# Running sums of a state-space scan sent through DRAM to all partitions, with the masks added on GpSimd

## What is computed

```python
def segsum_exp(a):
    cs = jnp.cumsum(a, axis=-1)
    diff = cs[..., :, None] - cs[..., None, :]
    mask = jnp.tril(jnp.ones((t, t), dtype=bool))
    return jnp.exp(jnp.where(mask, diff, -jnp.inf))
...
    xg = xs * dt[..., None]
    a = dt * a_neg
    cb = jnp.einsum('bclgn,bcsgn->bcgls', cc, bc)
    m_mat = cb[:, :, :, None] * segsum_exp(a)
    y_diag = jnp.einsum('bcgels,bcsgep->bclgep', m_mat, xg)
...
    y_off = jnp.einsum('bclgn,bcgepn,bcgel->bclgep', cc, prev_states, jnp.exp(a_cs))
    y = y_diag + y_off + d_skip * xs
    y = rmsnorm(y * silu(z), groups of 512) ; out = concat(attn, y) @ w_out
```

## Time and profile before

| | |
|---|---|
| median of 3 runs | 860.03 us (859.88 to 860.25) |
| profiled execution | 860.37 us |
| its span, first to last instruction | 858.3 us |
| PE busy | 850.3 us, 99% |
| PE weight loads busy | 707.6 us, 82% |
| DVE busy | 620.0 us, 72% |
| ACT busy | 534.6 us, 62% |
| POOL busy | 185.6 us, 22% |

### The profile page before, as it was taken

How to read it: one execution, slowest core, us unless ns; L and a number is a source line. 1 busy time by engine, 2 the same in 40 slices (tenths; PEclk the granted TensorE clock), 3 DMA queues, 4 the chain that set the end, 5 groups by cost and what they waited for, 6 DMA issues and landing times.

```text
span 858.3 us, 13054 instructions
## 1 busy us (share of the span) xinstructions
PE 850.3 (99%) x4645; PEld 707.6 (82%) x4645; DVE 620.0 (72%) x1125; ACT 534.6 (62%) x1031; POOL 185.6 (22%) x176
## 2 busy tenths in 40 slices
PE   9999999999999999999999999999999999999996
PEld 7877888778887888888888888877888888888885
DVE  6867866678776797778887546576797678877544
ACT  7668466765887864655565434787874655665432
POOL 0212053110152430023222000152330022222001
PEclk9999999999999999999999999999999999999999
DMA  9813563445434336655555555444336555555631
GB/s 316 293 56 127 178 203 130 148 147 176 157 139 147 110 140 217 203 177 185 195 190 178 222 196 172 151 147 141 107 145 220 186 185 196 189 177 180 230 107 50
DMA packets 94948, 146.21 MB, mean 170 GB/s; under 512 B 6564, under 2 KB 55204, under 8 KB 94884
## 3 DMA queue, kind: packets, MB, share of 16 engines
q1 hardware_dynamic: 92852, 139.58, 48.6%
q0 software_dynamic: 1296, 4.72, 1.7%
q10 hardware_dynamic: 736, 1.07, 0.3%
HBM read 144.32 MB, written 1.05 MB: 169 GB/s over the span
## 4 chain that ended last, share of the span: by engine, by line
PE 99%; issue 0%; POOL 0%; DVE 0%; ACT 0%; POOLq 0%; DVEq 0%
PE bank L1335 57%; PE bank L1291 17%; PE bank L1294 9%; PE bank L1217 6%; PE bank L1492 2%; PE bank L1420 1%; PE bank L1396 1%; PE bank L1393 1%; PE bank L1423 1%; PE bank L1222 0%; PE bank L1238 0%; PE bank L1236 0%; PE bank L1233 0%; PE bank L1482 0%; PE bank L1499 0%; PE bank L1460 0%
## 5 line engine op out<-in xcount | busy, mean ns | idle before, releaser
L1126 DVE TENSOR_TENSOR lo<-raw,hi 128x1024 fp32r<-128x1024 f32 x242 | 299.8, 1262 | 102.1 <-ACT hi L1511 101.7
L1511 ACT ACTIVATE hi<-raw 128x1024 fp32r<-128x1024 f32 (+1 forms) x258 | 266.7, 1058 | 126.8 <-PE bank L1335 68.2
L1335 PE MATMUL bank<-hi,xT 128*128 128x512 f32 (+2 forms) x800 | 252.0, 386 | 0.0
L1335 PEld LDWEIGHTS bank<-hi,xT 128*128 128x128 f32 x800 | 147.2, 188 | 30.9 <-issue 4.3
L1291 PE MATMUL bank<-xT,hi 128*128 128x512 f32 x640 | 171.8, 394 | 0.0
L1335 PE MATMUL bank<-lo,xT 128*128 128x512 f32 (+2 forms) x400 | 151.0, 378 | 0.0
L1291 PEld LDWEIGHTS bank<-xT,hi 128*128 128x128 f32 x640 | 110.6, 188 | 16.3
L1335 PE MATMUL bank<-hi,hT 128*128 128x512 f32 x348 | 107.8, 389 | 0.0
L1294 PEld LDWEIGHTS bank<-xT,lo 128*128 128x128 f32 x640 | 95.6, 189 | 11.9
L1294 PE MATMUL bank<-xT,lo 128*128 128x256 f32 x640 | 99.1, 281 | 0.0
L1335 PEld LDWEIGHTS bank<-lo,xT 128*128 128x128 f32 x400 | 75.4, 189 | 12.1
(11 more groups left out here) (284 smaller groups left out, 1119.0 us busy)
## 6 DMA issues: line engine op xcount, KB each, us to landing
raw<-in_w_in SPq DMA_DIRECT2D x26, 1024.0 KB, 4.9
raw<-in_w_gate SPq DMA_DIRECT2D x44, 512.0 KB, 3.7
raw<-in_w_up SPq DMA_DIRECT2D x44, 512.0 KB, 4.7
raw<-in_w_down SPq DMA_DIRECT2D x22, 1024.0 KB, 4.8
raw<-in_w_out SPq DMA_DIRECT2D x20, 1024.0 KB, 5.0
raw<-in_w_in_b SPq DMA_DIRECT2D x10, 1024.0 KB, 5.0
raw<-in_w_in_a SPq DMA_DIRECT2D x7, 1024.0 KB, 7.8
raw<-in_w_in_a SPq DMA_DIRECT2D x8, 256.0 KB, 5.2
```

Source lines behind the costliest of these rows:

```text
L1126: return engine.tensor_tensor(lo[r][:, cols], raw[c.i % RAW][:, cols], hi[r][:, cols].bitcast(F32), ALU.subtract)
L1335: last = nc.tensor.matmul(bank[:, 0:wd], still[a], mv[r][:, off:off + wd], start=c.first and i == 0 and j == 0, stop=(c.last or c.closes a ...
L1511: nc.scalar.activation(hi[c.i % SPLIT][:, cols], raw[c.i % RAW][:, cols], ACT.Copy)\
```

## The change

The negative running sums are kept as 16 rows in f32 (`csum`, now [16, 2, 128]; `sums` loses the three bf16 parts and writes the rows with one DVE operation, and `soft3` writes dt * a once instead of three times with zeros beside it). SP writes them to DRAM (`rows_out`, behind the products of `x0 + 512`), and reads them back with eight DMAs per layer (`spread`), each of which puts four rows on all 128 partitions: 256 KB into one of now eight buffers MT0 to MT7. Six of them are issued ahead of the products of `z0`, two within the first chunk of `z0 + 512`. SP waits for the write, for the last transposes of the attention, and for the last convolution transposes ahead of the seventh.

A new step `cap` on POOL adds a mask (`later`, bf16: zero or 1e30) to each buffer, 128 x 512 at a time: groups (0,0) and (0,1) in the chunks of `z0`, groups (1,1) and (1,0) in the second place of `z0 + 512`, which in the list is behind the first `xback` and ahead of the second. `decay` is then only ACT's exponential, in place in MT, with scale -1 and `ncs` as the bias. The decay matmuls, their turns in the ring of banks, `picks` and its setup on DVE go away.

```diff
+    def rows_spread(groups):
+
+        for g, m in groups:
+            for i in range(2):
+                scan["spread", g, m, i] = sc.step("spread", q=i, mg=(m, g), layer=layer, att=a, before=scan.get(("conv", 2, 1)))
+
+    def caps(g, m):
+
+        for i in range(2):
+            scan["cap", g, m, i] = sc.step("cap", q=i, mg=(m, g), of=scan["spread", g, m, i], sums=scan["sums"])
+
     def decays(g, m):
         for i in range(2):
-            bk = sc.bank()
-            s = sc.step("decay", q=i, mg=(m, g), bank=bk, sums=scan["sums"])
-            bk.freed = (s, "scalar")
-            scan["decay", g, m, i] = s
+            scan["decay", g, m, i] = sc.step("decay", q=i, mg=(m, g), of=scan["cap", g, m, i])
...
     b = halves(sc, w_in, [(x0 + 512, 512)], do(conv_silu, 0), att(2) + do(conv, 1, 0), do(conv, 1, 1))
+    sc.step("rows_out", layer=layer, sums=scan["sums"])
     evac_x(b, 2)
     sc.goes_on(att(3))
     scan["gain"] = sc.gain(("ssm_norm", layer))
-    b = halves(sc, w_in, [(z0, 512)], do(conv_silu, 1), do(conv, 2, 0) + do(bback),
+    rows_spread(((0, 0), (0, 1), (1, 1)))
+    b = halves(sc, w_in, [(z0, 512)], do(conv_silu, 1), do(caps, 0, 0) + do(caps, 0, 1) + do(conv, 2, 0) + do(bback),
                do(back, 0) + do(conv, 2, 1))
     scan["z", 0] = evacs(sc, b, "ev_z", j=0, kind_of="h")
     sc.goes_on(do(conv_silu, 2))
-    b = halves(sc, w_in, [(z0 + 512, 512)], do(decays, 0, 0) + do(weigh, 0, 0),
-               do(decays, 0, 1) + do(weigh, 0, 1), do(scanned, 0, 0) + do(back, 1) + do(low_at_once))
+    b = halves(sc, w_in, [(z0 + 512, 512)], do(rows_spread, ((1, 0),)) + do(decays, 0, 0) + do(weigh, 0, 0),
+               do(caps, 1, 1) + do(caps, 1, 0) + do(decays, 0, 1) + do(weigh, 0, 1), do(scanned, 0, 0) + do(back, 1) + do(low_at_once))
     ev_z1 = evacs(sc, b, "ev_z", j=1, kind_of="h", what="copy")
     sc.goes_on(do(squared, 0, 0) + do(decays, 1, 1) + do(scanned, 0, 1))
...
-    csum = keep("csum", [P, M, P], BF16)
-    picks = keep("picks", [P, SH, P], BF16)
+    decays = keep("decays", [P, 2, 4, P])
+    decay_rows = nc.dram_tensor("decay_rows", (2, SH, M, P), F32, kind="Internal").ap()
...
+                if s.kind == "rows_out":
+                    ended(sp, s.sums, "vector")
+                    sp.dma_start(decay_rows[s.layer], Hb["csum"][:, :, :]).then_inc(rows_stored, 16)
+                if s.kind == "spread":
+
+                    n, (m, g) = s.i % 8, s.mg
+                    if n == 0:
+                        sp.wait_ge(rows_stored, 16 * (s.layer + 1))
+                        for x in s.att["flip"][-3:]:
+                            ended(sp, x, "tensor")
+                    if n == 6:
+                        ended(sp, s.before, "tensor")
+                    hh = 8 * g + 4 * s.q
+                    sp.dma_start(Hb[f"MT{n}"][:, :, :], decay_rows[s.layer, hh:hh + 4, m].partition_broadcast(P))\
+                      .then_inc(spread_in[n], 16)
...
-                    last = nc.tensor.matmul(bank[0:96, 64 + m * P:64 + (m + 1) * P],
-                                            Hb["da"][:, m, :, :].rearrange("p a s -> p (a s)"), upper,
+                    last = nc.tensor.matmul(bank[0:SH, 64 + m * P:64 + (m + 1) * P], Hb["da"][:, m, :], upper,
                                             start=True, stop=True)
...
-            elif s.kind == "decay":
-                m, g = s.mg
-                ended(pe, s.sums, "scalar")
-                bank = freed(pe, s.bank)
-                if s.i == 0:
-                    pe.wait_ge(picks_made, 1)
-                for i in range(4):
-                    hh = 8 * g + 4 * (s.q % 2) + i
-                    last = nc.tensor.matmul(bank[:, i * P:(i + 1) * P], picks[0:KSEL, hh, :], csum[0:KSEL, m, :],
-                                            start=True, stop=True)
-                last.then_inc(sem["decay", "tensor"], 1)
...
-                act.wait_ge(sem["decay", "tensor"], s.i + 1)
-                if s.i >= 4:
-                    act.wait_ge(sem["diag", "tensor"], s.i - 3)
+                ended(act, s.of, "gpsimd")
                 for i in range(4):
                     hh = 8 * g + 4 * (s.q % 2) + i
-                    last = nc.scalar.activation(Hb[f"MT{s.i % 4}"][:, i, :], psum[4 + s.bank.at][:, i * P:(i + 1) * P],
-                                                ACT.Exp, bias=Hb["ncs"][:, m, hh:hh + 1])
+                    mt = Hb[f"MT{s.i % 8}"][:, i, :]
+                    last = nc.scalar.activation(mt, mt, ACT.Exp, scale=-1.0, bias=Hb["ncs"][:, m, hh:hh + 1])
                 done(last, s)
...
+            if s.kind == "cap":
+
+                m, g = s.mg
+                pool.wait_ge(spread_in[s.i % 8], 16 * (s.of.layer + 1))
+                ended(pool, s.sums, "vector")
+                mt = Hb[f"MT{s.i % 8}"][:, :, :]
+                nc.gpsimd.tensor_tensor(mt, mt, spread(Hb["later"][:, :].unsqueeze(1), [P, 4, P]), ALU.add)\
+                  .then_inc(sem["cap", "gpsimd"], 1)
...
-                copy, left = nc.vector.tensor_copy, bank[:, 64:64 + M * P].rearrange("p (m l) -> p m l", l=P)
-                chained(copy(csum[0:96, :, :], left[0:96]))
-                chained(tt(left[0:96], left[0:96], csum[0:96, :, :], ALU.subtract))
-                copy(csum[32:64, :, :], left[32:64])
-                chained(copy(csum[64:96, :, :], left[64:96]))
-                chained(tt(left[64:96], left[64:96], csum[64:96, :, :], ALU.subtract))
-                done(copy(csum[64:96, :, :], left[64:96]), s)
+                if s.i == 0:
+
+                    ts(Hb["later"][:, :], upper, NEG, -NEG, ALU.mult, ALU.add)
+                done(ts(Hb["csum"][:, :, :].rearrange("p m l -> p (m l)"), bank[0:SH, 64:64 + M * P], -1.0, None, ALU.mult), s)
```

More of the change, by code:

```diff
@@ L50 @@
 SINE_AT, TABLES_AT, ALOG_AT = 13, 21, 18
-PICKS_AT = 24
 POOL_SPLITS = 6
@@ L70 @@
 C_MASK = C_KEEP
[L71 to L75, removed]
+C_ALL = C_MASK + 2 * QC
 def constants():
@@ L104, in constants @@
             c[:, at:at + P] = np.where(x, 0.0, NEG)
[L105 to L109, removed]
     return c
@@ L586, in conv @@
         bk = sc.bank()
-        s = sc.step("conv", j=j, u=u, bank=bk, ev=scan["ev", j], layer=layer,
+        s = scan["conv", j, u] = sc.step("conv", j=j, u=u, bank=bk, ev=scan["ev", j], layer=layer,
                     conv=scan["silu", j - 1] if j else None)
@@ L895 @@
     "bback": ("tensor", "scalar", "vector"), "xback": ("tensor", "scalar", "gpsimd"),
-    "decay": ("tensor", "scalar"), "weigh": ("vector",), "diag": ("tensor",), "off": ("tensor",),
+    "decay": ("scalar",), "cap": ("gpsimd",), "spread": (), "rows_out": (), "weigh": ("vector",), "diag": ("tensor",), "off": ("tensor",),
     "join": ("vector",), "ysquare": ("scalar",), "ynorm": ("vector",), "final": ("vector",), "scaled": ("vector",), "part_sum": ("vector",), "tail_square": ("vector",), "tail_added": ("vector",), "pool_scaled": ("gpsimd",),
@@ L1039, in plan @@
             put("MT3", [P, 4, P], where=e)
-            put("da", [P, M, 3, M * SH], where=b["z_at"])
+            b["MT4"], b["MT5"] = decays[:, 0], decays[:, 1]
+            e = put("MT6", [P, 4, P], where=b["xin_at"])
+            put("MT7", [P, 4, P], where=e)
+            put("da", [P, M, SH], where=b["z_at"])
+            put("csum", [SH, M, P], where=b["z_at"] + 4 * (M * D - M * P))
             put("xs", [P, M, SSM])
@@ L1047, in plan @@
                 e = put(name, [P, M, SH], where=e)
+            put("later", [P, P], BF16, where=e)
             e = small_at
@@ L1084, in build @@
     warm_up = nc.alloc_semaphore("warm_up")
-    picks_made = nc.alloc_semaphore("picks_made")
+    rows_stored = nc.alloc_semaphore("rows_stored")
+    spread_in = [nc.alloc_semaphore(f"spread_in{i}") for i in range(8)]
     gain_in = nc.alloc_semaphore("gain_in")
@@ L1435, in _ @@
                 for m in range(M):
-                    c0, da = SH * m, Hb["da"][:, m, 0, SH * m:SH * (m + 1)]
+                    c0, da = SH * m, Hb["da"][:, m, :]
                     nc.tensor.matmul(bank[:, c0:c0 + SH], upper, da, start=True, stop=True)
-                nc.tensor.matmul(bank[:, 32:32 + SH], spread(ones[:, :], [P, P]), Hb["da"][:, 0, 0, 0:SH], start=True, stop=True)
+                nc.tensor.matmul(bank[:, 32:32 + SH], spread(ones[:, :], [P, P]), Hb["da"][:, 0, :], start=True, stop=True)
                 for m in range(M):
-                    last = nc.tensor.matmul(bank[0:96, 64 + m * P:64 + (m + 1) * P],
-                                            Hb["da"][:, m, :, :].rearrange("p a s -> p (a s)"), upper,
+                    last = nc.tensor.matmul(bank[0:SH, 64 + m * P:64 + (m + 1) * P], Hb["da"][:, m, :], upper,
                                             start=True, stop=True)
@@ L1491, in _ @@
                     c0 = (4 * (s.q % 2) + i) * HD
-                    last = nc.tensor.matmul(bank[:, c0:c0 + HD], Hb[f"MT{s.decay.of.i % 4}"][:, i, :],
```

(15 more changed lines are left out.)

## The result

The kernel after takes 861.08 us (median of 10 runs, 860.75 to 863.02); the kernel before, run beside it, 859.97 (10 runs, 859.59 to 860.29). The ratio is 1.0018, with a 95% interval of 1.0009 to 1.0026: about 1 us slower, although 64 matmuls have gone. The forecast was 863.0 in a range of 857.8 to 866.0. The profiled execution took 860.79, with a span of 858.6.

What follows compares the result with a forecast made beforehand. PE was taken to bound the kernel. Profiled 860.37, less 3.7 for removed matmuls, plus 3.7 + 3.0 of waiting at the two quarters, gives 863.4; the median lies 0.34 lower, so 863.0, range 857.8 to 866.0.

Steps and rivals of the forecast that it cites:

- the first rival: POOL additions take 1.04 or find more gaps; DVE 0.9 to 1.7 late, total 860.4 to 861.8; chance 0.20.
- the forecast's own band: Total time 861.8 to 866.0, from 1.04 against 1.3 per addition and none to all gaps filled; chance 0.47.
- What bounds the kernel, and where the gain goes: PE, busy 850.3 of 858.3 us, bounds; the removed 3.7 us disappears in waits at the first normed quarter.
- the two transposes that were named: PE's transposes of each layer's first normed quarter, waiting on DVE; about 3.4 us per layer including the wait at `off`.
- DVE and POOL take turns, `weigh` too: In the SSM scans, POOL additions and DVE's SBUF-to-SBUF work exclude each other; `weigh` shows 1.2 to 1.9 instead of 0.69.
- The size of DVE's lateness: Between the two `xback` steps, three additions of 1.2 effective, less gaps, make DVE 2.3 us late.
- the walk: Step-by-step timing of four additions, `weigh` steps and splits from 290.97 on; quarter ready about 313.5 instead of 311.17.
- The lateness stays at 2.3: From the split of 296.70 to the quarter, DVE takes turns with the second `xback` as before, keeping its 2.3 us lateness.
- The additions in the chunks of z0 cost nothing: Each layer's first four additions, 5.1 us, fit POOL's 12.20 us idle ahead of `xback`; counted as nothing.
- Exponentials in place: ACT's scan exponentials take 2.5 (2.2 to 2.9) against 2.18; without additions they eat 0.3 to 0.7 per layer.
- The added wait at the bank of `off`: PE's first `off` matmul waits for the bank the first `join` empties; PE stands here first, correspondingly less at the quarter.
- Spreads: On SP's DMA queue, 1.5 MB delay a weight load to about 276; counted nothing, upper bound 1 to 2 us per layer.

Runs made afterwards that it cites:

- e4: Kernel after, with the additions of (1,1) moved to the z0 chunks and PE's products of (1,1) put ahead of the first quarter's transposes: 857.50 us, ratio 0.9972.
- e2: Kernel after without any of the sixteen POOL additions, ACT taking the exponential straight from the spread data: 858.96 us, ratio to before 0.9994.
- e1: Kernel after with the additions of group (1,1) moved to the z0 chunks, behind those of (0,1): 858.76 us, ratio to before 0.9990.
- e9: Kernel after, unchanged, run again for a second trace: 862.67 us.
- e10: Kernel after, unchanged, run again for a third trace: 863.14 us.
- e7: Kernel before with eight useless POOL additions per layer between the two xback steps: 870.77 us, ratio 1.0129.
- e8: Kernel before with six useless POOL additions per layer between the two xback steps: 870.41 us, ratio 1.0121.

## Why the prediction was right, and where it was not

*The number:* 861.08 lies in the range because the range takes in the first rival too. The side that I held most likely, slower than 861.7 (0.52), did not come, and the forecast's own band, 861.8 to 866.0, was missed.

*What bounds the kernel, and where the gain goes:* right. PE lost 3.4 us of busy time for the 3.7 counted, and stood 3.0 at the two transposes that were named (L1238 on DVE L2301). But I had PE standing for about 3.4 per layer in all; it was 1.5 at the quarter and 0.46 at `diag`. e4 shows the reverse: without the stands most of the gain is there.

*DVE and POOL take turns, `weigh` too:* right, and now shown in rows: 3.12 for two `weigh` steps beside additions, 1.28 for two without. The Trainium skill (SBUF — State Buffer, section "SBUF: two separate sides") says so for any DVE operation with two SBUF inputs against a GpSimd operation that reads SBUF; the trace agrees for scalar_tensor_tensor.

*The size of DVE's lateness:* this is the term that was mis-sized. I had 2.3 us at the last `weigh`, staying at 2.3 up to the quarter. Measured by the mark it is 1.8 and 1.2. Half a microsecond went because the walk took three additions at 1.2 each, 3.6, of what DVE loses to them; by the rows they cost DVE (3.12 - 1.28) + (2.17 - 1.22) = 2.8, some 0.93 each, and DVE's idle times took up about 1.0 of that (1.3 in the walk). (Undisturbed, an addition takes 1.16, between the 1.04 of the nearest row and the 1.28 that I took.) Another 0.6 went because the lateness does not stay: the second `xback` on POOL begins when ACT has made its input, whatever DVE does, so a later DVE meets fewer and other POOL steps. The last multiplication of the join took 1.42 before and 0.69 after, while the addition ahead of it took longer (0.88 before, 1.21 after); and the 0.24 that DVE idled ahead of that join is used up. My sentence "The lateness stays at 2.3" was a guess in the middle of a walk. By the measured 1.2, each layer ends 0.4 late, 860.8 in all: that is the first rival (0.9 to 1.7 late, 860.4 to 861.8), to which I gave 0.20 and the forecast 0.47.

*The additions in the chunks of z0 cost nothing:* right. POOL was idle for 5.75 ahead of `xback` after them, and e2, without them, is no faster than e1.

*Exponentials in place:* the duration was right (2.4 to 2.5 taken as 2.5, gave 2.2 to 2.9). That they would eat 0.3 to 0.7 of a layer's gain without the additions was wrong: e2 has them without that cover, and the quarter moves by 0.13.

*The added wait at the bank of `off`:* wrong place. No stand shows there. PE stands at the second `diag`, for the second `weigh` (0.46 per layer): the walk had that `weigh` near 294.7 and did not ask when PE wants its result.

*Spreads:* right as far as it goes: no wait for a spread or for a load of these layers appears among the waits of ACT and POOL in after. The load issued next to them, at 268.00, landed 7.1 later, at 275.1; I had about 276, and ACT takes it up at 278.67.

*What was missing altogether:* a stand of PE was counted at its own length. In three of ten runs it cost 1.7 to 2 more, by the clock as the traces e9 and e10 show it. No case of the prediction held that.

## What to carry to other kernels

Where one engine is busy for 99%, a saving on it is worth only the slack of the next thing it waits for; read that slack (here 0.82 us) before counting the saving, and then either bring the other engine forward or put work that is ready in front of the wait, as e4 does with both (857.50 against 859.92). Work "on an idle engine" is not free if it reads the memory that a busy engine reads: where it stands in the order decides between no cost that shows (six of eight additions) and 1.1 us of lateness per layer (the last two). To compare lateness between two traces, measure from an event that both share.

## What the runs showed of the hardware that I had not expected

- TensorE's granted clock can fall to 0.50 behind a stand of only 1.5 us, some 2 us after PE is busy again and for about 3.4 us (two of the three traces of after). Behind stands of 2.8 to 2.9 it was at 0.50 at once and for over 6 us in the first layer, and in the second only 1.8 us later and for 3.4 (e7, e8).
- Adding a bf16 row that is repeated over four heads to an f32 buffer of 128 x 512 takes POOL 1.16 us undisturbed (a pair takes 2.28 to 2.29).
- An exponential of eight 128 x 128 pieces takes 2.45 us in place in SBUF, 2.18 from PSUM to SBUF.
